# Modulation weights moved from the prologue into later stages, conditional row transfers, and one rotation of three buffers for all expert blocks

## What is computed

```
for l in range(DEPTH):
    mod = c_act @ ada_w[l] + ada_b[l]
    sh1, sc1, g1 = mod[:, None, 0:D], mod[:, None, D:2 * D], mod[:, None, 2 * D:3 * D]
    sh2, sc2, g2 = mod[:, None, 3 * D:4 * D], mod[:, None, 4 * D:5 * D], mod[:, None, 5 * D:6 * D]
    h = rmsnorm(x, norm1_g[l]) * (1.0 + sc1) + sh1
    x = x + g1 * token_mix(h, ...)
    h = rmsnorm(x, norm2_g[l]) * (1.0 + sc2) + sh2
    x = x + g2 * grouped_moe(h, ...)
```

```
# two experts per token, from one group of four; combine holds their weights, 0 elsewhere
for e in range(N_EXPERTS):
    he = jax.nn.silu(t @ w_gate[e]) * (t @ w_up[e])
    y = y + combine[:, e:e + 1] * (he @ w_down[e])
```

## Time and profile before

| | us |
|---|---|
| median of 3 runs | 2097.59 (2095.94 to 2101.18) |
| the profiled execution, time | 2101.24 |
| its span, first to last instruction | 2099.4 |
| PE busy | 1885.4 (90%) |
| DVE busy | 582.5 (28%) |
| ACT busy | 534.3 (25%) |
| POOL busy | 81.1 (4%) |
| moved by DMA | 546.30 MB, 260 GB/s on average |

### The profile page before, as it was taken

The page is one execution under the profiler, slowest core; times in us unless marked ns, Lnnn a source line. Parts: engine busy times, 40 slices in busy tenths (PEclk is TensorE's granted clock), DMA queues, the critical chain, the costliest instruction groups (busy, mean ns, idle before and its releaser), DMA issues.

```text
span 2099.4 us, 26022 instructions
## 1 busy us (share of the span) xinstructions
PE 1885.4 (90%) x10456; PEld 1309.5 (62%) x10456; DVE 582.5 (28%) x1087; ACT 534.3 (25%) x923; POOL 81.1 (4%) x137
## 2 busy tenths in 40 slices
PE   4799998588999599999499998599979999987998
PEld 1467767333333467768333333477779997677998
DVE  1134142200000235141200000323155542235554
ACT  1001231111111200231111111315045442444543
POOL 0000000010110100000011111000000000000000
PEclk8899999699999799999699999699989999998999
DMA  9976443699998756452699996677954553222450
GB/s 390 427 312 249 182 185 130 260 424 396 416 417 344 291 191 248 185 198 116 245 424 415 421 416 276 270 311 293 367 207 165 196 205 125 90 121 110 170 200 20
DMA packets 54478, 546.30 MB, mean 260 GB/s; under 512 B 7280, under 2 KB 11632, under 8 KB 23408
## 3 DMA queue, kind: packets, MB, share of 16 engines
q1 hardware_dynamic: 42656, 505.66, 59.9%
q0 software_dynamic: 11728, 39.33, 4.9%
HBM read 590.58 MB, written 27.79 MB: 295 GB/s over the span
## 4 chain that ended last, share of the span: by engine, by line
PE 83%; DMA 7%; DVE 4%; issue 2%; DVEq 1%; ACT 1%; POOL 1%; SPq 0%; POOLq 0%; ACTq 0%; PEldq 0%
PE bank L836 26%; PE bank L1113 14%; PE bank L1137 7%; PE bank L801 6%; PE bank L802 6%; PE bank L803 6%; PE bank L846 4%; DMA ring<-in_w_up 3%; DMA ring<-in_ada 3%; PE bank L1247 2%; PE bank L950 1%; PE bank L907 1%; PE bank L1316 1%; PE bank L1230 1%; PE bank L1087 1%
## 5 line engine op out<-in xcount | busy, mean ns | idle before, releaser
L836 PE MATMUL bank<-h_t,ring 128*128 128x256 f32 (+1 forms) x1824 | 409.5, 386 | 27.3 <-DVE h_t L1930 24.0
L836 PEld LDWEIGHTS bank<-h_t,ring 128*128 128x128 f32 (+1 forms) x1824 | 348.4, 192 | 84.5 <-issue 22.9
L801 PE MATMUL bank<-split_x,split_w 128*128 128x256 f32 x1024 | 289.3, 283 | 1.1 <-DVE split_w L2198 1.1
L802 PE MATMUL bank<-split_x,split_w 128*128 128x256 f32 x1024 | 288.9, 282 | 0.0
L803 PE MATMUL bank<-split_x,split_w 128*128 128x256 f32 x1024 | 288.7, 282 | 0.0
L1113 PE MATMUL bank<-ring,h_t 128*64 128x512 f32 x1024 | 233.3, 607 | 13.5 <-DMA ring<-in_w_up 9.8
L801 PEld LDWEIGHTS bank<-split_x,split_w 128*128 128x128 f32 x1024 | 194.9, 190 | 2.9 <-DVE split_w L2198 2.9
L802 PEld LDWEIGHTS bank<-split_x,split_w 128*128 128x128 f32 x1024 | 194.9, 190 | 0.0
L803 PEld LDWEIGHTS bank<-split_x,split_w 128*128 128x128 f32 x1024 | 194.8, 190 | 0.0
L2198 DVE TENSOR_TENSOR split_w<-ring,split_w 128x1024 fp32r<-128x1024 f32 x128 | 156.3, 1225 | 92.0 <-ACT split_w L1642 91.7
L1113 PEld LDWEIGHTS bank<-ring,h_t 128*64 128x64 f32 x1024 | 84.0, 140 | 147.7 <-issue 145.9
(11 more groups left out here) (306 smaller groups left out, 1795.0 us busy)
## 6 DMA issues: line engine op xcount, KB each, us to landing
ring<-in_ada SPq DMA_DIRECT2D x48, 2048.0 KB, 13.8
ring<-in_w_gate SPq DMA_DIRECT2D x32, 2048.0 KB, 12.7
ring<-in_w_up SPq DMA_DIRECT2D x32, 2048.0 KB, 17.6
ring<-in_w_down SPq DMA_DIRECT2D x32, 2048.0 KB, 15.2
ring<-in_mlp_w SPq DMA_DIRECT2D x32, 2048.0 KB, 8.7
ring<-in_w_in SPq DMA_DIRECT2D x16, 2048.0 KB, 8.7
mix<-in_w_gate SPq DMA_DIRECT2D x14, 2048.0 KB
mix<-in_w_up SPq DMA_DIRECT2D x14, 2048.0 KB
```

The source lines that it names most:

```text
L801: pe.matmul(out, hi, x_hi, start=start, stop=False, **kw)
L802: pe.matmul(out, hi, x_lo, start=False, stop=False, **kw)
L836: ins = pe.matmul(bank[0:width, place * T:place * T + T], w_ap[:, k, c0:c0 + width], rhs[:, k, :], start=(k == 0), stop=(k == nk - 1))
```

## The change

Four edits.

1. `EARLY` = 4 of a layer's 12 modulation units (shift and scale of the first norm) are made ahead of the layer, the other eight (`LATE`) within it. In the prologue 4 units are left. A layer of the first network still has twelve: eight of its own ("ada now") and four of the next ("ada next"). The recurrent layer has its own eight besides the 16 it had, 24 in all, in groups of two to four. Two condition tiles (`cond_now`, `cond_next`) replace one; "columns" writes `mod` directly, and in the recurrent layer it stands between the first and the second half of the last output part, ahead of the sums into `x_t`.
2. The expert blocks are one list, extra block x behind experts 2x+2 and 2x+3, and block n uses buffer n mod 3. The third buffer loads after `yb3`, before the experts begin. Down weights are issued behind the next block's gate and up. On PE `gate_up(n)` always stands before `down(n-1)`. The order of the pairs' transposes is set by `PAIR_BEHIND`.
3. The row load of a pair of extra blocks and the stores of an extra block are conditional on its use. POOL reads seven flags into registers for it, after the scatter and ahead of the first pair's load. The rows for these results are set to zero once.
4. The zeroing of `expert_token_rows` starts at the step "cross" in layer 0, no longer at the end of the prologue. The tiles `tok` and `xsq` move behind the third buffer.

```
-            for u in range(12):
-                if u >= SLOTS:
-                    sp.wait_ge(P0.sem, P0.at(f"row{u - SLOTS}"))
+            for u in range(EARLY):
                 sp.dma_start(flat_slot(u, SLOT), unit_rows(ada[0], D * 512 * u, SLOT))...
-                if u == 1:
+                if u == 0:
                     sp.dma_start(x_t, xT).then_inc(x_loaded, 16)
...
-            for u in range(AU):
-                if u == 5:
+            for u in range(EARLY):
+                if u == 2:
                     pe.wait_ge(A0.sem, A0.at("sq"))
...
+BUFFERS = 3
+BLOCKS = [(e, False) for e in range(2)]
+for x in range(XB):
+    BLOCKS += [(2 * x + 2, False), (2 * x + 3, False), (x, True)]
...
+for n in range(NB):
+    if n + 2 < NB and BLOCKS[n + 2][1] and pair_of(n + 2) not in PAIRS:
+        PAIR_BEHIND[n] = pair_of(n + 2)
+    elif n + 1 < NB and not BLOCKS[n][1] and BLOCKS[n][0] % 2 and BLOCKS[n][0] + 1 < NE:
+        PAIR_BEHIND[n] = f"xp{BLOCKS[n][0] + 1}"
...
# SP
+                for n, j in ((1, 1), (1, 2), (0, 0), (0, 1), (2, 0), (2, 1), (2, 2), (0, 2), (1, 0)):
+                    if n == 2:
+                        if j == 0:
+                            sp.wait_ge(DV.sem, DV.at("yb3", l))
+                    else:
+                        sp.wait_ge(PE.sem, PE.at(LAST_USE_OF_SLOT[3 * n + j], l))
+                    load(n, (j,))
...
+                    load(n, (0, 1), which)
+                    if held:
+                        load(*held)
+                    held = (n, (2,), which)
...
# PE
+                for n in range(NB):
+                    gate_up(n, range(0, 6))
+                    if n:
+                        hidden_rows(n - 1)
+                    gate_up(n, range(6, KT))
+                    if n in PAIR_BEHIND:
+                        token_rows(PAIR_BEHIND[n])
+                    if n:
+                        down(n - 1)
...
# POOL
+                used = [pool.value_load(extra[0:1, XB + i:XB + i + 1], min_val=0, max_val=1) for i in range(XB)]
...
+                        pool.dma_start(raw, x_rows[at:at + P, :], cond=used[i]).then_inc(raw_full, 16)
...
+                pair_rows("xp0")
+                done = 0
+                for r, name in enumerate(PAIRS[1:]):
+                    behind = [n for n in PAIR_BEHIND if PAIR_BEHIND[n] == name][0]
+                    pool.wait_ge(MP.sem, MP.at(PAIRS[r], l))
+                    pair_rows(name)
+                    while done < behind:
+                        store(done)
+                        done += 1
+                while done < NB:
+                    store(done)
+                    done += 1
...
# recurrent layer
-R_RING = [0, 1, "mod0", "mod1", 2, "mod2", "mod3", 3, "mod4", "mod5", 6, 7, "mod6", "mod7", 4, "mod8", "mod9", 5,
-          "mod10", "mod11", 8, "mod12", "mod13", 9, "mod14", "mod15", 10]
+for name, n in [("xr1", 2), ("xr5", 3), ("gelu1", 4), (f"ri{LT - 1}", 4), ("gelu5", 4), ("part0", 4), ("part1", 3)]:
+    MODS_AFTER[name] = range(first, first + n)
+    first += n
...
+R_RING = [0, *mods_after("xr1"), 1, 2, *mods_after("xr5"), 3, *mods_after("gelu1"), 6, 7, *mods_after(f"ri{LT - 1}"),
+          4, 5, *mods_after("gelu5"), 8, *mods_after("part0"), 9, *mods_after("part1"), 10]
```

More of the change, by code:

```diff
@@ L105, with mod_unit @@
 LAST_USE = [LAST_USE[u] if u in range(len(UNITS)) else u for u in RING]
-RING_UNITS = [UNITS[u] if u in range(len(UNITS)) else ("ada", D, 512 * int(u[3:]), 512) for u in RING]
+def mod_unit(j):
+    return ("ada now", D, 512 * (j + EARLY), 512) if j < LATE else ("ada next", D, 512 * (j - LATE), 512)
+RING_UNITS = [UNITS[u] if u in range(len(UNITS)) else mod_unit(int(u[3:])) for u in RING]
 STATIC_IN = [len(range(s, len(RING), SLOTS)) for s in range(SLOTS)]
@@ L388 @@
 R_DVE = (["condition", "lambda", "x0", "x1", "x2", "x3", "h1 0", "h1 1"] + [f"conv{i}" for i in range(6)]
[L389 removed]
+         + ["ix0", "ix1", "ix2", "u0", "u1", "u2", "y0", "y1", "y2", "columns"] + [f"out{i}" for i in range(4)] + H2
          + ["h lo0", "h lo1"])
@@ L576, in program @@
         ys_full = [sem(f"expert_rows_of_tokens{i}_full") for i in range(TT)]
-        P0 = Steps(sem("prologue_pe"), [f"row{u}" for u in range(5)] + ["norm"] + [f"row{u}" for u in range(5, AU)]
-                   + ["columns"])
+        P0 = Steps(sem("prologue_pe"), ["row0", "row1", "norm", "row2", "row3", "columns"])
         A0 = Steps(sem("prologue_act"), ["c", "sq", "trig", "lb", "rows"])
@@ new lines, in _ @@
+                for n, j in ((1, 1), (1, 2), (0, 0), (0, 1), (2, 0), (2, 1), (2, 2), (0, 2), (1, 0)):
+                    if n == 2:
+                        if j == 0:
+                            sp.wait_ge(DV.sem, DV.at("yb3", l))
+                    else:
+                        sp.wait_ge(PE.sem, PE.at(LAST_USE_OF_SLOT[3 * n + j], l))
+                    load(n, (j,))
+                held = None
+                for n in range(BUFFERS, NB):
+                    i, is_extra = BLOCKS[n]
+                    which = None
+                    if is_extra:
@@ L730, in _ @@
                 else:
-                    name, _, nk, r0, c0, n = unit
-                    src = w["ada"][3] if name == "ada" else w[name][0]
+                    name, which, nk, r0, c0, n = unit
+                    src = w["ada"][which] if name == "ada" else w[name][0]
                     at = r0 * D if name == "lru_w_out_2" else D * c0
@@ L1245, in _ @@
                 for o in range(KT):
+                    if u == 2 and o == KT // 2:
+                        b = r_job("columns")
+                        pe.wait_ge(AR.sem, AR.at("mod rows"))
+                        to_columns(b, cqkv).then_inc(PR.sem, PR.one("columns"))
                     for k in range(n):
@@ L1252, in _ @@
                     ins.then_inc(PR.sem, PR.one(f"part{u}"))
-                    mod_row(12 + 2 * u)
-                    mod_row(13 + 2 * u)
-            b = r_job("columns")
-            pe.wait_ge(AR.sem, AR.at("mod rows"))
-            to_columns(b, cqkv).then_inc(PR.sem, PR.one("columns"))
+                    for j in MODS_AFTER.get(f"part{u}", ()):
+                        mod_row(j)
             sum_squares(r_job("norm2"), h_t, KT, AR, SQ2).then_inc(PR.sem, PR.one("norm2"))
@@ L1346, in _ @@
         def _(pool):
-            pool.wait_ge(P0.sem, P0.at(f"row{AU - 1}"))
+            pool.wait_ge(PE.sem, PE.at("cross"))
             pieces = ROWS * D // (P * T)
@@ new lines, in store @@
+                        if is_extra:
+                            pool.dma_start(to, block, cond=used[i]).then_inc(out_stored[n % 2], 16)
+                        else:
+                            pool.dma_start(to, block).then_inc(out_stored[n % 2], 16)
+                pair_rows("xp0")
[7 more added lines that the diff above has]
+                        done += 1
```

332 lines of the change are left out of this document (153 added, 179 removed).

## The result

| | median us (lowest to highest, runs) | profiled span us |
|---|---|---|
| before | 2098.52 (2095.94 to 2101.18, 4) | 2099.4 |
| after | 2140.22 (2139.20 to 2144.16, 4) | 2137.8 |

The changed kernel is slower: 1.020 times the time before, interval 1.0184 to 1.0216, +41.7 us. The prediction had the sign and named the wait that does it, but said 2118 us with a range up to 2132; 2140 lies 8 us above that range.

What follows compares the result with a forecast made beforehand. DMA was taken to bound the prologue, PE layer 1's experts and the recurrent layer. Terms -39 + 0.5 + 15.2 - 18 + 10 + 56 - 4 = +20.7 us on 2101.24 gave 2121.9, less 3.6: 2118 us, range 2070 to 2132.

Steps and rivals of the forecast that it cites:

- Prologue: Start to first projection: eight modulation units fewer at 4.89 us a matrix, taken as -39 us.
- Recurrent layer: Recurrent layer: eight more units add +14.2 us of PE time, taken as +15.2 with short waits at landings.
- Flag reads: Between scatter and first row load: POOL's seven reads at 0.72 us each, +5.0 us a layer, +10 in all.
- Experts' end: After the last expert block, now an unused extra one with skipped stores: -2 us a layer, -4 in all.
- Token rows: Experts of both layers: PE waits for row loads issued behind POOL's stores, with slow products after long waits, +56 us.
- Third buffer: Experts' weights: nine matrices loaded ahead instead of six remove weight waits, -18 us in layer 0, about nothing in layer 1.
- The rival that said the third buffer would do nothing: Experts: weight waits stay, since buffers are shared at the same distance as before; about 2128 us, chance 0.09.
- the expert terms: Both layers' expert stages: +56 us for token rows and -18 for weights, together +38.
- The mixers: Mixers 0 and 1: predicted +0.5 us.

Runs made afterwards that it cites:

- e1: Kernel before with the modulation edits alone, its expert loop kept: 2084.64 us, ratio 0.9932 to before.
- e3: Changed kernel with POOL's seven flag reads moved behind the first pair's row load: 2127.02 us, ratio 1.0132 to before.
- e9: Changed kernel without the conditions on POOL's token-row loads and stores and without the flag reads: 2136.80 us, ratio 1.0177 to before.
- e4: Changed kernel with a second token-row tile, flag reads behind the first two loads, and loads ahead of stores: 2076.07 us, ratio 0.9888 to before.
- e7: e4 with only half of every expert's down matrix loaded, so the output is not the layer's: 2062.17 us in one run.
- e5: Kernel before with only the tile hidden_sb widened from 512 to 600 words: 2104.95 us, ratio 1.0040 to before.
- e10: Kernel before with hidden_sb at 520 words instead of 512, one run: last stretch 552.8 us.
- e13: Kernel before with hidden_sb at 536 words instead of 512, one run: last stretch 566.6 us.
- e12: e4 with hidden_sb at 616 words instead of 600: 2068.81 us, ratio 0.9855 to before.
- e2: Changed kernel with POOL issuing the next pair's row load before the block's store, not behind it: 2092.26 us, ratio 0.9963 to before.

## Why the prediction missed

**Prologue: right.** -40.8 for -39. The lead from the last unit's end (31.81 + 1.92) to the first projection is 6.9 us as said; most of the difference is the last unit's product, which took 1.92 us where it had taken 3.22.

**Recurrent layer: right in mechanism, 1.4 us short.** e1 has 128 more products of modulation there, 42.7 us in place of 29.1: +13.6 for the +14.2 of PE time. The rest are two short waits, the first without a releaser in the profile; the changed kernel shows

```profile
1435.76 27.00 PE L1259 MATMUL bank<-mix,ring 128*128 128x256 f32 x124 [1.53 <-issue]
...
1471.23 9.12 PE L878 MATMUL bank<-h_t,ring 128*128 128x256 f32 x41 [1.47 <-DMA ring<-in_lru_w_in]
```

**Flag reads: right.** +8.6 for +10; e3 takes 4.5 and 4.1 away. A read costs 4.3 / 7 = 0.6 us on POOL, not SP's 0.72.

**Experts' end: right.** -5.3 for -4, and e9 puts it down to the skipped stores.

**Token rows: right in mechanism and place; the sum's +56 measured +49.7.** That is the changed kernel against e4: 20.6 us in layer 0 and 29.1 in layer 1. The waits were 50.2 us, 44 were predicted: the long ones as said (8.3, 7.1, 9.3, 8.6, 7.0 for 8, 8, 7.5, 8, 8), the three short ones 3.1 to 3.7 in place of 1.5. In layer 1 PE was busy for 271.07 against 263.89 us, so the slow products cost 1.8 us a wait on average over all four, not 2.4 behind the long ones alone. In layer 0 part of the price is paid already: e4 has 11.0 us of waits for weights there, and 4.7 us of slow products behind them (268.80 us busy against e7's 264.09). That the term came out near is partly luck. Waits and slow products behind them were 50.2 + 15.7 = 66 us in the changed kernel (15.7 is 272.57 - 264.09 and 271.07 - 263.89), ten more than said, and some 16 of them only stood where waits for weights would have been, an overlap that the sum did not have.

**Third buffer: the step that failed.** The term -18 measured -0.5 (e4 against before). I read the waits of the earlier trace rows rightly as weights that come too late, and took the three extra matrices loaded ahead for their cure. But the kernel before had the same nine buffers, and its three matrices were on their way at 399.96, in the very row I read the earlier trace rows. Loaded earlier they only left DMA with a share of 0.16 in the first 10 us of e4's experts, where it had 1.00 before. At a share of 0.99 over the whole 107 us there was nothing to be gained but by fewer bytes; e7 has fewer, and gained the 15 us. The rival that said the third buffer would do nothing had 0.09 and was priced at 2128, "less what both waits share", so even it counted too little. With 0 for -18 and +49.7 for +56 the expert terms give the +49.2 that both stages show, 11.2 more than the 38 predicted.

**The last stretch: not in the sum.** +7.6 us, through a tile of 88 more words (e5: +7.6 in median time). I had costed the second condition tile's instructions and not its place.

**The rest.** The mixers gave 1.9 more than said, which is within their scatter. Recurrent layer +1.4, prologue -1.8, flag reads -1.4, ends -1.3: in all 17.7 us of span (the parts are rounded). The median adds 4.4, since I took off 3.6 for the profiled run of before, while that of after lies 0.8 under its median.

## What to carry over

Where two waits stand in one stretch, don't credit the removal of one and charge the other: each hides behind the other, and what stays is the tighter supply. Before a load made earlier is counted as a gain, count the buffers on both sides and ask what DMA will do in the time that it leaves; where its share is 0.99 it takes fewer bytes, not another order. A load that feeds the bottleneck goes ahead of the stores in its queue and has a tile of its own, and when a tile's size is changed, look at where the tiles behind it come to lie.

## What the hardware showed

- The same 1536 products of an MLP took 182 to 187 us as the tiles behind `hidden_sb` moved (176 in one MLP of e10, unexplained): most at a multiple of 128 bytes (e5, e13, after), 2.2 to 2.8 us less at 32 and 96 (4.3 in the second MLP of before), and 3.5 to 4.3 less at 64 (e12 and the first MLP of e10), some 1% to 2%. In the whole kernel's time only the step to a multiple of 128 was measured beyond its interval (e5). Why the place matters stays open.
- A row load of 512 KB lands 3.5 us after its issue at best, 11.0 among weights (e2) and 13.5 among weights behind two stores (after). The weights do most of it; the last two are one load each.
- After waits as short as 3.1 us PE's products were slow for a while, 1.8 us of extra time a wait in layer 1. The slow stretch did not always begin at once: behind the 3.20 at 581.52 and the 3.74 at 1161.95 the transposes took 1.09 us as ever, and the down products behind them 5.35 in place of 3.65.
- A skipped transfer costs 0.04 us on POOL to issue, and two of them with what lies between 0.4.
